# Six changes in the order of work of a two-block transformer kernel, with latent and context query tiles taken alternately in layer 0

## What is computed

```python
def first_block(x, mem, ...):              # 512 tokens, 256 memory rows, width 1024
    mem_n = rmsnorm(mem, mem_norm_w)
    for i in range(2):
        h = rmsnorm(x, norm_w[i])
        # i == 0: gated linear attention (block A); i == 1: dilated attention in 3 groups (block B)
        mix, q_mem, gate = mixer(h)
        mem_o = memory_attention(q_mem, mem_n, w_memkv[i])
        x = x + (concatenate([mix, mem_o]) * silu(gate)) @ w_out[i]
    return rmsnorm(x, final_norm_w)

def _layer(x, xc, ...):                    # second block, twice; xc: 256 context rows
    h, hc = modulated norms of x and xc
    a_out = neighbourhood attention(h) + context keys
    # differential attention, 4 heads, keys are 512 latent + 256 context
    w = softmax(q1 @ k1.T) - lam * softmax(q2 @ k2.T);  b_out = rms(w @ v)
    c_out = conv over 31 taps, layer norm, silu
    y = concatenate([a_out * silu(g_a), b_out * silu(g_b), c_out * silu(g_c)]) @ w_out
    # in layer 0 the context rows go through the same steps (update_ctx)
    return x + gate * rms(y), xc + gate_c * rms(yc)
```

## Time and profile before

| | us |
|---|---|
| runs | 1659.37, 1659.65, 1657.1 |
| median | 1659.37 |
| span of the profiled execution | 1658.7 |
| PE busy | 1600.2 |
| DVE busy | 981.3 |
| ACT busy | 665.9 |
| POOL busy | 139.1 |

### The profile page before, as it was taken

How to read it: one execution, slowest core, us unless ns; L and a number is a source line. 1 busy time by engine, 2 the same in 40 slices (tenths; PEclk the granted TensorE clock), 3 DMA queues, 4 the chain that set the end, 5 groups by cost and what they waited for, 6 DMA issues and landing times.

```text
span 1658.7 us, 23002 instructions
## 1 busy us (share of the span) xinstructions
PE 1600.2 (96%) x8918; PEld 1279.5 (77%) x8918; DVE 981.3 (59%) x1788; ACT 665.9 (40%) x1323; POOL 139.1 (8%) x192
## 2 busy tenths in 40 slices
PE   6999999999999999999999999989998999999898
PEld 5977777887888888888888778865656887788676
DVE  1346464456466555665447786565665467876774
...
GB/s 289 78 39 89 102 140 96 114 82 136 174 157 121 157 188 138 148 141 84 76 114 97 51 52 39 91 93 58 1 26 95 42 162 91 58 39 128 52 14 38
DMA packets 171236, 161.35 MB, mean 97 GB/s; under 512 B 40359, under 2 KB 154265, under 8 KB 171097
## 3 DMA queue, kind: packets, MB, share of 16 engines
...
## 4 chain that ended last, share of the span: by engine, by line
PE 80%; DVE 11%; ACT 4%; issue 3%; DMA 1%; POOL 0%; SPq 0%; ACTq 0%; POOLq 0%; DVEq 0%
PE psum L2577 44%; PE psum L2548 12%; PE psum L2609 6%; PE psum L3091 5%; PE psum L2600 4%; PE psum L3089 2%; PE psum L2735 2%; PE psum L2658 2%; DVE arena L1980 1%; PE psum L2639 1%; DVE arena L1953 1%; DVE psum L2406 1%; ACT arena L1848 1%; DVE stat L2403 1%; DVE arena L2424 1%
## 5 line engine op out<-in xcount | busy, mean ns | idle before, releaser
L2577 PE MATMUL psum<-hT_r,wring_r 128*128 128x512 f32 x1696 | 573.4, 392 | 6.0 <-ACT arena L1545 3.0
L2577 PEld LDWEIGHTS psum<-hT_r,wring_r 128*128 128x128 f32 x1696 | 318.4, 188 | 81.1 <-issue 14.1
L2577 PE MATMUL psum<-arena_r,wring_r 128*128 128x256 f32 (+1 forms) x1360 | 358.0, 332 | 2.4 <-DVE arena_r L2116 2.4
L1545 ACT ACTIVATE arena<-psum 128x512 f32<-128x512 f32 (+6 forms) x256 | 149.3, 612 | 428.0 <-PE psum L2577 240.3
L2577 PEld LDWEIGHTS psum<-arena_r,wring_r 128*128 128x128 f32 x1360 | 217.8, 190 | 27.7 <-issue 3.9
L2548 PE MATMUL psum<-arena 128*128 128x96 f32 (+9 forms) x1460 | 216.1, 362 | 12.0 <-ACT arena L1885 4.5
L2577 PE MATMUL psum<-arena_r 128*128 128x512 f32 (+1 forms) x720 | 224.3, 350 | 0.0
L2548 PEld LDWEIGHTS psum<-arena 128*128 128x128 f32 (+5 forms) x1460 | 156.9, 187 | 58.8 <-issue 32.0
L2577 PE MATMUL psum<-hT_r,arena_r 128*128 128x512 f32 x448 | 177.7, 397 | 0.9 <-ACT arena L1545 0.9
L2609 PE MATMUL psum<-ident,arena 128*128 128x128 f32 (+3 forms) x1056 | 137.7, 277 | 21.0 <-DMA arena<-in_g_post 10.6
L2609 PEld LDWEIGHTS psum<-ident,arena 128*128 128x128 f32 (+3 forms) x1056 | 118.3, 142 | 42.7 <-issue 16.5
...
## 6 DMA issues: line engine op xcount, KB each, us to landing
...
arena<-x_dram SPq DMA_DIRECT2D x3, 2048.0 KB, 13.5
...
```

Of the source, the lines that this page charges most:

```text
L1545: return nc.scalar.activation(out, in_, ACT.Copy, scale=scale)
L2577: ins_ = nc.tensor.matmul(b[0:hi.shape[2], 0:width], w[:, k], v[:, k], start=k + p == 0, stop=(k, p) == (KT - 1, 2))
```

## The change

1. *Start.* Only four vector loads (identity, memory norm weight, c, c_ctx) count for `vecT 0`, the other three go to `vecT 1`. DVE scales the memory tiles ahead of the copy of the vectors. The first memkv chunk comes as two DMAs, and `memkv` waits block by block and runs keys and values side by side.
2. *Block A.* `Ao` takes tiles in pairs (0, 2), (1, 3). `wide` of wout goes before `qm A`, and `AoT` behind it. The first two jobs of `wout A` leave blocks 6 and 7 to the end.
3. *Block B.* `gate B 4` goes behind `qm B`. At the end `modulation()` goes behind `gate B 5`, and the products of gates 6 and 7 with the memory output behind the last `BT`.
4. *Into a layer.* `nkc` waits for each pair of blocks, three of the four tiles of `hT` are turned between its jobs (`early_rows`), and layer 0's end forms the norms of tile 2 ahead of the last tile's turning. `nq` goes before `nv`, and POOL's additions of the bias (`self_bias`, three in a layer's first call) go with `nq`.
5. *Neighbourhood stage.* Where the next gate is layer 0's `gatec` or layer 1's `gate`, it comes ahead of the softmax of unit u + 2, and not behind it.
6. *Differential stage.* In layer 0 the tiles are taken in the order 0, 4, 1, 5, 2, 3 and not 4, 5, 0, 1, 2, 3; in both layers `half(1)` goes into `beside(0)`, and what stood there goes one place further on. Some scratch areas move with it.

```diff
@@ -122,2 +122,3 @@
 
+NEXT_NORMS = (("C1", 0), ("c1", 0), ("C1", 1), ("c1", 1), ("C1", 2), ("C1", 3))
 FINAL_NORMS = (("F", 0), ("F", 1), ("C0", 0), ("C0", 1), ("F", 2), ("C0", 2), ("F", 3), ("C0", 3))
@@ -168,7 +169,7 @@
     add("a", "gate", "A", 5)
+    add("", "wide", "wout", "A", 0, (0, 1))
+    add("av", "qm", "A")
     add("v" * 6, "AoT")
-    add("av", "qm", "A")
     add("a" * 8, "mS", "A")
     add("a", "gate", "A", 6)
-    add("", "wide", "wout", "A", 0, (0, 1))
     add("a", "gate", "A", 7)
@@ -200,5 +201,6 @@
     add("v" * 8, "hT", "B")
-    for i in range(5):
+    for i in range(4):
         add("a", "gate", "B", i)
     add("av", "qm", "B")
+    add("a", "gate", "B", 4)
     add("a" * 8, "mS", "B")
@@ -225,7 +227,7 @@
         else:
-            modulation()
             for n in range(2):
                 add("", "wide", "wout", "B", n, (0, 1, 2, 3))
                 add("", "wlo", "wout", "B", n, (0, 1, 2, 3))
             add("a", "gate", "B", 5)
+            modulation()
             add("", "Bw", h)
@@ -252,4 +254,4 @@
         add("av" * 3, "nvF", l)
+        add(lat_ctx * 3, "nq", l)
         add("aaaavv", "nv", l)
-        add(lat_ctx * 3, "nq", l)
         neighbourhood(add, l)
@@ -276,3 +278,3 @@
                     add("a", "cT", l, h)
-        turns = [("k", t) for t in (0, 1, TT, 2, 3, TT + 1)] + [("q", t) for t in diff_tiles(l)]
+        turns = turn_order(l)
 
@@ -304,14 +306,15 @@
         add("aa" * (1 + both), "cvZ", l)
-        half(1)
 
         def beside(n):
 
             if n == 0:
-                add(*values[1])
+                half(1)
                 turn(5)
                 add("vv", "dv", l, 0)
             elif n == 1:
+                add(*values[1])
+                turn(6)
                 half(2)
+            elif n == 2:
                 add("vv", "dv", l, 1)
-                turn(6)
             elif n == 3:
@@ -398,9 +401,12 @@
 
-    def filled(n):
-
-        for _ in range(n):
-            step = gates.pop(0)
-            add(*step)
-            if step[1:] == ("gate", f"C{l}", NH // 2 - 1):
-                add("", "gS", l, 0)
+    def filled():
+
+        step = gates.pop(0)
+        add(*step)
+        return step[1:] == ("gate", f"C{l}", NH // 2 - 1)
+
+    def silu(due):
+
+        if due:
+            add("", "gS", l, 0)
 
@@ -417,8 +423,8 @@
 
-    filled(1)
+    silu(filled())
     for u in range(DEPTH):
         add("aa", "nS", l, *units[u])
         if u < 2 and l == 0:
             softmax(u)
-        filled(1)
+        silu(filled())
         if u < 2 and l:
@@ -432,6 +438,13 @@
             add("", "nW", l, *units[u + 1])
-        softmax(u + 2)
-        if l and u:
-            product(u - 1)
-        filled(1)
+        if gates[0][1] == ("gate" if l else "gatec"):
+            if l and u:
+                product(u - 1)
+            due = filled()
+            softmax(u + 2)
+        else:
+            softmax(u + 2)
+            if l and u:
+                product(u - 1)
+            due = filled()
+        silu(due)
         add("", "taps", l, ("n", u), 2 - l)
@@ -448,11 +461,14 @@
         return range(BANKS - 1)
-    if key[2] == "k" or key[3] >= TT:
-        return range(BANKS - 1)
-    slot = (6 + key[3] + CT * (key[1] == 0)) // 2 + (key[0] == "dX")
+    slot = turn_order(key[1]).index(key[2:]) // 2 + (key[0] == "dX")
     return (range(BANKS - 1), (4, 5, 6), (4, 6))[max(slot, 4) - 4]
 
 
 def diff_tiles(l):
 
-    return ([TT + t for t in range(CT)] if l == 0 else []) + list(range(TT))
+    return [0, TT, 1, TT + 1, 2, 3] if l == 0 else list(range(TT))
+
+
+def turn_order(l):
+
+    return [("k", t) for t in (0, 1, TT, 2, 3, TT + 1)] + [("q", t) for t in diff_tiles(l)]
 
@@ -522,10 +538,13 @@
         add("", "yo", l, last, half, 0)
+    if l == 0:
+        add("", "yx", l, before)
     add("", "oN", l, last)
+    if l == 0:
+        add("", "nx", before)
     add("v", "doT", l, last)
     if l == 0:
         add("vvvv", "hcT", 1)
-    add("", "yx", l, before)
+    else:
+        add("", "yx", l, before)
     add("v", "yo", l, last, 0, 1)
-    if l == 0:
-        add("", "nx", before)
     add("v", "yo", l, last, 1, 1)
...
@@ -783,2 +801,3 @@
         w_full = [sem(f"w_full{i}") for i in range(WSLOTS)]
+        kv_first = sem("kv_first")
         vecs_in, vecs2_in, gla_in, const_in, mem_first, x_in = (sem(n) for n in (
...
@@ -1276,3 +1296,3 @@
                 sp.dma_start(crows, ins["conv_w_2"].rearrange("l k c -> (l k) c")).then_inc(vecs2_in, 16)
-                assert 16 * (n_vec + 1) == VECS2_IN, n_vec
+                assert 16 * (n_vec + 4) == VECS2_IN, n_vec
                 for q, name in enumerate(("diff_lq1_2", "diff_lk1_2", "diff_lq2_2", "diff_lk2_2")):
@@ -1303,3 +1323,6 @@
                         read_by_pe(sp, last)
-                    for i in range(loads(arg)):
+                    if arg == 0:
+                        sp.dma_start(slot(arg)[:, 0:KT // 2], src[:, 0:KT // 2]).then_inc(kv_first, 16)
+                        sp.dma_start(slot(arg)[:, KT // 2:], src[:, KT // 2:]).then_inc(w_full[0], 16)
+                    for i in range(loads(arg) if arg else 0):
                         dst, part = (slot(arg), src) if loads(arg) == 1 else (slot4(arg)[:, :, i], src[:, :, i])
@@ -1493,4 +1516,5 @@
                     pool.dma_start(nv_dram[l].rearrange("(t p) c -> p t c", p=P), vnat).then_inc(nv_saved, 16)
+                elif kind == "nq":
                     for j in range(NH // 2):
-                        self_bias(pool, l, 0, j)
+                        self_bias(pool, key[1], 0, j)
                 elif kind == "nS":
...
@@ -1566,8 +1589,8 @@
             act.dma_start(ident[:, :], consts["ident"]).then_inc(vecs_in, 16)
+            rows(V_MEM, ins["mem_norm_w"].rearrange("(r c) -> r c", c=P), KT)
             rows(V_C, ins["c_2"][0].rearrange("(r c) -> r c", c=P), KT)
             rows(V_C + KT, ins["c_ctx_2"].rearrange("(r c) -> r c", c=P), KT)
-            rows(V_MEM, ins["mem_norm_w"].rearrange("(r c) -> r c", c=P), KT)
-            rows(V_NORM, ins["norm_w"].rearrange("l (r c) -> (l r) c", c=P), 2 * KT)
-            rows(V_GPRE, ins["g_pre_2"].rearrange("l (r c) -> (l r) c", c=P), 2 * KT)
-            rows(V_GPOST, ins["g_post_2"].rearrange("l (r c) -> (l r) c", c=P), 2 * KT)
+            for r, name in ((V_NORM, "norm_w"), (V_GPRE, "g_pre_2"), (V_GPOST, "g_post_2")):
+                act.dma_start(vrows2[r - V_EARLY:r - V_EARLY + 2 * KT, :],
+                              ins[name].rearrange("l (r c) -> (l r) c", c=P)).then_inc(vecs2_in, 16)
 
...
@@ -2000,8 +2023,8 @@
                 if kind == "vecT" and key[1] == 0:
+                    for t in range(CT):
+                        norm_scale("m", t)
                     free(nc.vector.tensor_copy(vec[:, 0:V_EARLY], full(dve, key, 0)[:, 0:V_EARLY]))
                     evacuated(dve, key)
                     nc.vector.tensor_reduce(group_sum, ident[:, :].rearrange("p (g c) -> p c g", c=GROUP)[:, 0:2], AX_X,
                                             ALU.add).then_inc(sums_ready, 1)
-                    for t in range(CT):
-                        norm_scale("m", t)
                 elif kind == "vecT":
...
@@ -2202,7 +2225,2 @@
                         free(nc.vector.tensor_copy(branch[:, 6 + j], full(dve, key, j)[:, :]))
-                elif key[:2] == ("gate", "B") and key[2] >= 6:
-                    evacuated(dve, key)
-                    evacuated(dve, ("mPV", "B"))
-                    i = key[2]
-                    mul(branch[:, i], branch[:, i], bgates[:, i - 6]).then_inc(mem_gated, 1)
                 elif kind == "mPV":
@@ -2322,2 +2340,7 @@
                                                    full(dve, key, i)[:, 0:n * P].rearrange("p (n q) -> p n q", q=P)))
+                    if h == BH - 1:
+                        evacuated(dve, ("mPV", "B"))
+                        for i in (6, 7):
+                            evacuated(dve, ("gate", "B", i))
+                            mul(branch[:, i], branch[:, i], bgates[:, i - 6]).then_inc(mem_gated, 1)
                 elif kind == "BPV":
@@ -2570,5 +2593,5 @@
                 new = {("gate", "B", 0): ("hT", "B")}.get(key)
-                if key[0] == "nkc" and i == 0:
-                    evacuated(pe, ("hcT", key[1]), 3)
                 for k in blocks:
+                    if key[0] == "nkc" and i == 0 and k % 2 == 0:
+                        evacuated(pe, ("hcT", key[1]), k // 2)
                     if new and i == 0:
...
@@ -2588,2 +2611,4 @@
                 for i, k in enumerate(order):
+                    if part is not None and (k >= 6) != part:
+                        continue
                     q = k // 2
@@ -2612,2 +2637,11 @@
                 pe.wait_ge(xn_ready, norm_pe[ph])
+
+            def early_rows(key):
+
+                pe.wait_ge(xn_ready, norm_pe[key[1]] - 1)
+                src = norms[key[1]][1]
+                for k in range(HT_BANKS):
```

(57 more changed lines are left out.)

42 lines of the change are left out of this document (23 added, 19 removed).

## The result

The changed kernel takes 1674.4 us (1673.5 to 1674.8), the one before, run beside it, 1659.5: a ratio of 1.0084, 95% interval 1.0072 to 1.0096. It is slower, by 15 us, and outside the range of the prediction (1649 to 1667).

A forecast was written before the change was run, and what follows sets the result against it. TensorE (PE), busy 1600.2 of 1658.7 us, was taken to bound the kernel. Gains of 15.5 and costs of 14.9 gave net -0.6, a span of 1658.1 and a forecast of 1658.8 us; 8 in 10 range 1649 to 1667.

The forecast's parts named there:

- Gate B 4: Block B: ACT waits for a weight load before evacuating gate B 4, PE stops in mS B; +11.5 (8.6 to 13).
- The start: Kernel start: four vector loads land earlier than seven, so the memory projection begins at 13.5, not 17.6; -5.1 (-2.5 to -6.5).
- Ao: Block A: tiles in pairs, so matmul shapes change places four times a head, not eight; -1.5 (0 to -2.9).
- the end of A: End of block A: reordered weight halves and late blocks 6, 7 cover waits of 0.83 and 1.83; -1.7 (-0.5 to -2.2).
- the first of the two cases that the prediction left open: Ao: changing the tiling mode drains TensorE, making the pairing worth up to 2.9; with no drain, nothing.
- The differential stage: Layer 0: waits 8 to 9.5, or 7 with a clock fall, against 8.4, +0.7; layer 1: 5.1 against 2.9, +2.0.
- The entry to a layer: Into the second block (layer 0): +0.7 (-0.6 to +2.0); layer 0 to 1: most of a 2.44 wait goes, -1.9.
- the early turning: Layer entry: three of four tiles turned between nkc jobs; DVE is the late engine, so by itself 0 to -0.6.
- the bias additions: Layer entry: POOL's additions moved to nq's place lengthen DVE splits beside them; +0.7 (-0.6 to +2.0).
- The Trainium skill's rule on the shared port: Layer entry: GpSimd and VectorE's shared port locks for a whole instruction; with it the bias move could cost 2.0, without it nothing.
- The neighbourhood stages: Both layers: the gate evacuation no longer stands behind exponentials on ACT; -3.3 and -1.3, together -4.6 (-3.0 to -5.2).
- (c): Rival: slower, both layers' differential openings stall and the clock falls there too; 1669 us, chance 0.24.

The follow-up runs named there:

- e3: The changed kernel with gate B 4 ahead of qm B again, nothing else: 1664.2 us, ratio 1.0020 to the kernel before.
- e1: The changed kernel with half(1) and all steps between the differential items put back in both layers, tile alternation kept: 1656.2 us, ratio 0.9976 to the kernel before.
- e9: The changed kernel with half(1) alone put back ahead of the differential stage, the other moved steps still one item later: 1672.4 us, ratio 1.0066.
- e12: The changed kernel with half(1) left beside item 0, but values[1], half(2), dv 1 and turn 6 put back: 1663.8 us, ratio 1.0027.
- e6: e4 without the early turning: the three tiles of hT turned in hT's own step again, both layers: 1643.0 us, ratio 0.9895.
- e7: e4 with POOL's bias additions back in the nv step, and nv ahead of nq again in layer 1 alone: 1644.2 us, ratio 0.9901.
- e4: The changed kernel with half(1) and the steps moved with it, layer 0's old tile order and gate B 4 all put back: 1645.1 us, ratio 0.9907.

## Why the prediction was wrong

*Gate B 4* was right in mechanism, and in size with some luck: +10.5 against +11.5, with a wait of 6.90 where I said 7 to 8. The new idle time is 6.8 where I had 9.0, and the clock fall cost 3.7 where I took 2.5. The load landed 8.0 after gate B 4's end and not 8.8. e3 shows it.

*The start, Ao and the end of A* were right to within 1 each. At the start two errors leave the sum right: the loads landed 3 earlier than I took, and DVE, not they, holds memT. In the second head the matmuls of Ao take 3.3 us in pairs (147.10 to 150.44) and took 4.0 before (152.89 to 156.88), so the changes of place do cost time, the first of the two cases that the prediction left open; no run puts Ao back alone.

*The differential stage* is where it failed, in two steps. In layer 0 I wrote "8 to 9.5 in all, with no clock fall, or 7 with one". The waits of the first 60 us are 3.31, 0.94, 2.50, 0.99, 0.15, 0.86, 0.19 and 0.39, 9.3, as counted. But the choice between waits and clock was false: both came, twice, at 1085 and at 1110, 5.75 us of extra busy time (178.43 against 172.68 in e1), where 2.85 had been lost before. I had seen that waits of 5 us had brought one fall and yet priced more waits with none. In layer 1 the count itself was short: I had 5.1 for the waits of the opening, and they are 1.50, 2.88, 2.50 and 0.99, 7.9; and the clock cost 4.7 more on top, which stood at nothing in the sum. The wait of 2.50, the same in both layers, was not in my list: it comes from what was pushed one item later, which I took as mere order. It stands at the first product, dPV of item 0, which takes the bank that dv 1 had before it. Since the change dv 1 stands behind the scores of item 2, and DVE copies it only after that item's two row maxima:

```profile
1108.64 0.95 DVE L2481 TENSOR_REDUCE stat<-psum 128x1 f32<-128x768 f32 x1
...
1109.70 1.01 DVE L2416 COPY arena<-psum 128x256 f32<-128x256 f32 x2
```

(The view puts the wait down to ACT, whose exponential ended at the same moment; the kernel's list of banks names DVE's copy.) The wait stays in e9, where dv 1 stays late, and is gone in e1 and e12, where it is back; no run moves dv 1 alone. e12 shows that the pushed steps together carry 10.6 us by the medians, and 13.4 of the 17.2 in its trace.

*The entry to a layer:* +1.6 against +0.7, for the wrong reason. I wrote that the early turning would be "0 to -0.6" by itself and that the bias additions would cost. e6 and e7 show the reverse in layer 0. DVE is the late engine, as I wrote, and the turning does not delay it. The step that failed is to price the turning by DVE alone, and a fall of the clock at nothing: it takes 15 turns out of the time in which PE waits for DVE, and the clock falls behind the single wait of 2.10 that is left. The same turning took 1.2 of the gain in layer 1 (e6 against e4). That -1.9 came out as -0.4 there is the fall behind the same wait, which costs 1.6; in the traces without it the entry is at -2.0.

*The Trainium skill's rule on the shared port* (SBUF — State Buffer, SBUF: two separate sides) holds in kind, with 1.41 us for an operation that takes 0.69 elsewhere. But it explained no loss at the entries: e6 has such an operation of 1.53 at layer 0's entry and loses nothing, and e7 has none and loses 1.6. *The neighbourhood stages* gained 5.5 against 4.6, divided otherwise than I had it.

Of the rivals, (c) was the right one: slower, through stalls in the differential openings in both layers that bring the clock down. It had a chance of 0.24 and 1669, and even that is near partly by luck: 3.8 of its 10.2 above the forecast are for the start and the bias additions, where the runs show no such loss. For the two differential stages it had 9.3 (2.7 and one fall in each layer), and they cost 17.2, since the waits in layer 1 were more and the clock fell more often.
